# Differential attention: one 128-row score matmul per head over zero-padded keys, in place of two 64-row ones

## The reference, cut to what matters

```
q, k: (256 tokens, 16 heads, 2 maps, 64)      v: (256 tokens, 16 heads, 128)
s   = q . k                  # per map: 128 queries x 256 keys, contraction over 64
p   = softmax(s)             # per map
att = p[map 0] - lam * p[map 1]
o   = att . v                # 128 queries x 128
o   = rms_norm(o, subln) * (1 - lam_init);  m = o @ w_out
```

## Time and profile before

| what | value |
|---|---|
| median of 3 runs | 2351.28 us (2349.76 to 2351.54) |
| span of the profiled execution | 2349.4 us |
| median less that span | 1.9 us |
| mean granted TensorE clock | 0.994 |
| TensorE matmul, busy | 2296.2 us (98%) |
| TensorE weight load, busy | 1865.8 us (79%) |
| VectorE, busy | 1314.1 us (56%) |
| ScalarE, busy | 1027.8 us (44%) |
| GpSimd, busy | 249.6 us (11%) |
| score matmuls (L998), both layers | 192 instructions, 66.8 us busy |

### The profile page before, as it was taken

How to read it: one execution, slowest core, us unless ns; L and a number is a source line. 1 busy time by engine, 2 the same in 40 slices (tenths; PEclk the granted TensorE clock), 3 DMA queues, 4 the chain that set the end, 5 groups by cost and what they waited for, 6 DMA issues and landing times.

```text
span 2349.4 us, 27378 instructions
## 1 busy us (share of the span) xinstructions
PE 2296.2 (98%) x10337; PEld 1865.8 (79%) x10337; DVE 1314.1 (56%) x1308; ACT 1027.8 (44%) x1123; POOL 249.6 (11%) x241
## 2 busy tenths in 40 slices
PE   8999999999999999999999999999999999999997
PEld 6877777788888888888787777777888888888886
DVE  4567456655555555555745555667555555555555
ACT  5676444533333333333554445445333333333332
POOL 2463001300000000000421001005000000000002
PEclk9999999999999999999999999999999999999999
DMA  8544344555565555555464453545555555565552
GB/s 281 168 137 159 126 175 148 197 197 189 187 196 189 186 196 186 189 196 185 138 198 137 148 162 126 192 149 182 192 187 191 195 182 194 183 195 194 188 189 105
DMA packets 212263, 417.87 MB, mean 178 GB/s; under 512 B 12040, under 2 KB 12640, under 8 KB 211296
## 3 DMA queue, kind: packets, MB, share of 16 engines
q1 hardware_dynamic: 212192, 416.92, 54.0%
HBM read 414.79 MB, written 2.10 MB: 177 GB/s over the span
## 4 chain that ended last, share of the span: by engine, by line
issue 69%; PE 23%; POOL 3%; DVE 3%; DMA 1%; ACT 1%; SPq 0%; DVEq 0%; POOLq 0%; ACTq 0%
PE acc L917 18%; PE sc L998 2%; PE tp L931 1%; POOL yacc L1347 1%; DVE xs L1101 1%; DVE w_lo L1072 1%; DMA gq<-in_norm_ffn_post 1%; PE pv L1026 0%; POOL stage L1362 0%; POOL small L1339 0%; PE sc L976 0%; POOL gq L1411 0%; PE pv L976 0%; DMA gq<-in_norm_mix_post 0%; DVE h_lo L1077 0%
## 5 line engine op out<-in xcount | busy, mean ns | idle before, releaser
L1072 DVE TENSOR_TENSOR w_lo<-raw,w_hi 128x2048 fp32r<-128x2048 f32 x383 | 881.9, 2303 | 514.3 <-PE acc L917 497.1
L702 ACT ACTIVATE w_hi<-raw 128x2048 fp32r<-128x2048 f32 x383 | 734.0, 1917 | 761.5 <-PE acc L917 737.8
L917 PE MATMUL acc<-w_hi,h_hi 128*128 128x512 f32 x2240 | 888.5, 397 | 18.5 <-DVE h_lo L1077 18.5
L917 PE MATMUL acc<-w_hi,h_lo 128*128 128x512 f32 x2240 | 874.8, 391 | 0.0
L917 PE MATMUL acc<-w_lo,h_hi 128*128 128x512 f32 x2240 | 874.4, 390 | 0.0
L917 PEld LDWEIGHTS acc<-w_hi,h_hi 128*128 128x128 f32 x2240 | 422.4, 189 | 120.4 <-DVE h_lo L1077 24.7
L917 PEld LDWEIGHTS acc<-w_hi,h_lo 128*128 128x128 f32 x2240 | 421.9, 188 | 89.4
L917 PEld LDWEIGHTS acc<-w_lo,h_hi 128*128 128x128 f32 x2240 | 422.5, 189 | 84.1
L917 PE MATMUL acc<-w_hi,y_hi 128*128 128x512 f32 x832 | 325.8, 392 | 1.9 <-DVE y_lo L1077 1.9
L917 PE MATMUL acc<-w_hi,y_lo 128*128 128x512 f32 x832 | 323.9, 389 | 0.0
L917 PE MATMUL acc<-w_lo,y_hi 128*128 128x512 f32 x832 | 323.8, 389 | 0.0
(11 more groups left out here) (134 smaller groups left out, 1040.6 us busy)
## 6 DMA issues: line engine op xcount, KB each, us to landing
raw<-in_ffn_w_gate SPq DMA_DIRECT2D x88, 1024.0 KB, 5.1
raw<-in_ffn_w_up SPq DMA_DIRECT2D x88, 1024.0 KB, 5.1
raw<-in_ffn_w_down SPq DMA_DIRECT2D x88, 1024.0 KB, 5.0
raw<-in_od_w_in SPq DMA_DIRECT2D x48, 1024.0 KB, 5.1
raw<-in_ev_w_in SPq DMA_DIRECT2D x39, 1024.0 KB, 5.2
raw<-in_ev_w_out SPq DMA_DIRECT2D x16, 1024.0 KB, 5.1
raw<-in_od_w_out SPq DMA_DIRECT2D x16, 1024.0 KB, 5.0
xs<-in_x SPq DMA_DIRECT2D x4, 512.0 KB, 8.7
```

The costliest lines, as they stand in the source:

```text
L702: act.activation(w_hi[u % HI][:, :, :], raw[u % RAW][:, :, :], ACT.Copy).then_inc(hi_done, 1)
L917: mm = pe.matmul(acc[n % 2][t][:, :], operand(lhs, a, k, t), w[:, k, :], start=first and k == 0 and j == 0, stop=last and k == KT - 1 and ...
L1072: dve.tensor_tensor(w_lo[u % LO][:, :, :], raw[u % RAW][:, :, :], w_hi[u % HI][:, :, :].bitcast(F32), ALU.subtract).then_inc(lo_done, 1)
```

## The change

In layer 1 the keys are kept with both maps side by side along the columns: a buffer of 128 rows, 4 head blocks, 2 maps and 256 tokens, in which map 0's columns hold keys in rows 0 to 63 and zeros below, and map 1's columns zeros in rows 0 to 63 and keys below. With the queries of both maps stacked in 128 rows, one matmul of 512 columns gives both maps' scores. Two such buffers alternate by group: `gx` for groups 0 and 2, and `kz`, which takes the place of the two `kT` buffers (of the same size together), for groups 1 and 3. GpSimd fills both with zeros once, at slot 4 of layer 1. ScalarE copies each key transpose in two instructions of 64 rows. The joined matmul stands where `s0` stood; at `s` TensorE does nothing in layer 1. SP waits for the scores of group 2 before it loads gains into `gx`. Layer 0 is left as it is.

```diff
+KEYS_SLOT = 4
...
+    if layer == 1:
+        put(KEYS_SLOT, kind="zero_keys")
...
-        kT = [sb(f"kT{i}", [P, KT, T]) for i in range(2)]
+        kz = sb("kz", [P, KT, 2, T])
...
+        kz_flat = kz[:, :, :, :].rearrange("p k m t -> p (k m t)")
+        kT = [kz_flat[:, KT * T * i:KT * T * (i + 1)].rearrange("p (k t) -> p k t", k=KT) for i in range(2)]
         pre_gain, post_gain = gx[:, 0:D], gq[:, :]
+        keys = [gx[:, 0:D].rearrange("p (k m t) -> p k m t", k=KT, m=2), kz]
...
+                if b == 3:
+                    sp.wait_ge(s_done, 16 + 3 * HEADS_OF_GROUP)
...
+                    if task.layer == 1 and task.src == "k":
+                        keys_transposed(task)
+                        return
...
+            def keys_transposed(task):
+
+                t0, src = task.t * P, tp[task.e % 2]
+                act.wait_ge(keys_zero, 2)
+                for m in range(2):
+                    rows = slice(HD * m, HD * (m + 1))
+                    ins = act.activation(keys[task.g % 2][rows, :, m, t0:t0 + P], src[rows, :, :], ACT.Copy)
+                ins.then_inc(tp_free[task.e % 2], 1)
...
                     n, j = task.n, int(task.kind == "s")
+                    if j and task.layer == 1:
+                        return
...
-                    if task.layer == 0:
-                        r, kt, t = HD * (task.i % 2), task.i // 2, j
-                    else:
-                        r, kt, t = HD * j, task.i // 2, task.i % 2
+                    if task.layer == 1:
+                        kt, t = task.i // 2, task.i % 2
+                        pe.matmul(sc[:, :, :].rearrange("p m t -> p (m t)"), q[:, kt, t * P:(t + 1) * P],
+                                  keys[task.g % 2][:, kt, :, :].rearrange("p m t -> p (m t)"),
+                                  start=True, stop=True).then_inc(s_done, 1)
+                        return
+                    r, kt, t = HD * (task.i % 2), task.i // 2, j
...
+            def zero_keys():
+
+                pool.wait_ge(xg_done, 8 * 3)
+                pool.wait_ge(s_done, 16)
+                for buf in keys:
+                    pool.memset(buf[:, :, :, :], 0.0).then_inc(keys_zero, 1)
```

More of the change, by code:

```diff
@@ L464, in trunk @@
         halves = [flat[:, 2048 + 512 * i:2560 + 512 * i] for i in range(4)]
-        for buf in (qT[1], kT[1]):
-            flat_buf = buf[:, :, :].rearrange("p k t -> p (k t)")
+        for flat_buf in (qT[1][:, :, :].rearrange("p k t -> p (k t)"), kz_flat[:, KT * T:2 * KT * T]):
             halves += [flat_buf[:, 0:512], flat_buf[:, 512:1024]]
@@ L528, in trunk @@
         zero_done = sem("zero_done")
+        keys_zero = sem("keys_zero")
         par_T = sem("par_T")
@@ L1425, in task_of @@
                     convolve(task.i)
+                elif task.kind == "zero_keys":
+                    zero_keys()
                 elif task.kind == "heads":
```

## The result

The changed kernel takes 2327.94 us (median of 4, 2327.16 to 2329.11) against 2350.52 us (median of 4): ratio 0.9904, interval 0.9892 to 0.9916. The forecast was 2329.5, with a range of 2326 to 2336. Measured once more, beside a part of the experiments, it took 2328.28 us (2327.49 to 2329.22) against 2350.21, ratio 0.9906 (0.9891 to 0.9922). The profiled execution has a span of 2327.3 us, 22.1 us less than before, at a granted clock of 0.993.

A forecast was written before the change was run, and what follows sets the result against it. TensorE's queue was taken to bound layer 1: scores -23.0 us and key copies +1.2 us sum to -21.8 us, so 2351.3 us becomes 2329.5 us; 8-in-10 range 2326 to 2336 us.

The forecast's parts named there:

- Scores: Layer 1 score pairs: joining into 128 rows and 512 columns cuts 1.59 to 0.87 us, times 32, saving 23.0 us.
- A: Rival: half of the layer 1 score stall stays, one border pair per head, 2341.0 us; chance 0.07.
- C: Rival: 512-column float32 passes over 128 rows run at half rate, 1.74 us per pair, 2357.3 us; chance 0.03.
- B: Rival: TensorE waits instead for VectorE's round in group 3's score slots, up to 5 us, 2334.5 us; chance 0.06.
- D: Rival: joined matmul issues as more than two instructions; only kept 64-row halves leave time unchanged, 2351 + 1 us; chance 0.02.
- The copies: Split key copies delay head scaling after groups 0 and 1; TensorE waits 0.5 to 0.8 us, twice: +1.2 us.
- The fills: Two 128x2048 zero fills on GpSimd, 2.1 us each, hidden in its 15.20 us idle after group 0's query rotation.
- SP's wait: SP waits for group 2's scores before the gain load; 24 us to spare, about 20 after the change: costs nothing.
- VectorE's round: Group 3, the busiest case: VectorE needs 6.82 us against the new 7.03 us slot, so TensorE still sets the pace.
- The joined matmul's place: Score wholly at the first place: VectorE's 0.33 us wait before the maximum goes, nothing later by more than 0.16 us.
- the two maps don't run beside each other: Read from the earlier trace's 1.58 us pair against 0.87 us of columns, contradicting the skill's rule of parallel row tiles.
- a stall of the borders: Layer 1 scores: 0.72 us per pair beyond the columns, put down to the borders of the 64-row matmuls.

The follow-up runs named there:

- two-bank kernels: Kernel before, both 64-row scores at the first place, map 1's in the value product's bank: 2325.13 us; wait put back 2348.35 us, same rows instead 2337.95 us.

## Why the prediction was right, and where it wasn't

*Scores.* 0.87 us was taken and 0.86 measured, 32 times: 1.59 - 0.86 = 0.73, 23.4 us against the 23.0 of the sum. That it was the row form is shown from both sides, by the split 128-row matmuls (1.99 us again) and by the joined 64-row one (12 us back). Rivals A and C have nothing in the trace: the loads of the scores and the first of the transposes begin under the matmul before, and the two passes are 0.43 us apart. B has no wait for VectorE in group 3, and D is settled by the count, two instructions for each joined matmul.

*The copies.* The place, the chain and the two slots were right, the size was low: 0.98 us for each wait in place of 0.6, since half-height copies follow each other every 0.6 us and not every 0.5. That is 0.8 us more than the 1.2 of the sum, inside its bounds of 0 and 2. The total came out near the forecast partly by luck: in the two traces the scores give 23.3 us over the 32 pairs and the waits take 1.96, and the boundary, which the clock makes 0.58 us shorter in one of them, brings the difference back to 22.0; the spans differ by 22.1 (21.8 forecast).

*The rest.* The fills (1.84 us each, 2.1 forecast), SP's wait (26 us to spare) and VectorE's round (7.00 us, 7.03 forecast) were hidden as worked out. The joined matmul's place saves the 0.33 us ahead of the maximum for VectorE, and nothing at the end.

*The step that failed* is one that the sum didn't need: "the two maps don't run beside each other", from the four score instructions of the earlier trace rows, taken as against a rule. Those rows had a wait on a signal between the two matmuls, which the code shows (line 982 of the kernel before) and the prediction overlooked. Without it, and with two banks, they start 0.01 us apart. The Trainium skill, page "TensorEngine Tiling (Array Packing)", Key Properties, says that different tiles can load and multiply in parallel. The traces agree: 0.78 us for the pair against 1.20 on the same rows. The same list says that a change of tiling mode drains the engine. The 0.33 us for an entry and exit agrees with that, though the runs don't tell a drain from loads that merely aren't started early. Of the 0.72 us that the prediction called a stall of the borders, in a slot with all parts, it is two entries and exits (0.66) and about 0.07 beside them, which no run isolates; at the first head of a group it is one entry and exit (0.39) and 0.32 of signal (2.03 against 1.71 in the two-bank kernels with the wait and with the same rows), which is why both looked the same size.

*Loads.* The Trainium skill, page "TensorE: Matmul & The Clock Gate", Part 3, The mechanism, has a line that a weight load overlaps running matmuls only where the row groups differ. Taken by itself it is contradicted again, by the load at 1525.98 under the product of 1525.97, both over 128 rows; the paragraph ahead of that line also lets a load into the background weight buffer go ahead, and with that the trace agrees.

## What to carry to other kernels

Read starts, not busy time: subtract a slot without the operation from one with it, and compare the rest with the columns; what is left over is what a change of form can give. A matmul of few rows between full ones pays 0.33 us to enter and leave here, so either fill the rows with zeros, or put matmuls of different rows beside each other, in different banks and with no wait between, which was the better by 3 us here, needs no padded buffer and no split copies. Before a trace is held against a rule of overlap, look in the code for a wait that would hide it.

## What the runs showed that I had not expected

Two 64-row float32 matmuls on different rows start 0.01 us apart and share their columns' time, 0.78 us for the pair, where a wait on the first one's signal makes 1.53. A signal from TensorE to itself costs 0.33 us even between 128-row matmuls (1.65 against 1.32 us). And a stretch of some 3 us at half the granted clock cost 0.6 us or nothing, by whether it stood after a wait of TensorE or before one that could take it up. A difference of 0.6 us between two traces, in a part that the change doesn't touch, is therefore no effect of the change until more traces show it.
